# A two-layer hybrid block on one core: another order for the filters, twelve places for the second layer's expert weights, and branch products of split operands

## The reference

```python
def hyena_filter_spectrum(n, w1, b1, freq, w2, b2, w3):
    ...
    hh = jnp.sin(fr * (z @ w1.astype(f32) + b1.astype(f32)))
    hh = jnp.sin(fr * (hh @ w2.astype(f32) + b2.astype(f32)))
    hh = (hh @ w3.astype(f32)).reshape(n, HY_ORDER, 2, BRANCH_WIDTH)
    hh = hh * jnp.exp(-t * deltas)[:, None, None, :]
    fwd, bwd = hh[:, :, 0], hh[:, :, 1]
    buf = jnp.concatenate([fwd, jnp.zeros((1, HY_ORDER, BRANCH_WIDTH), f32), bwd[:0:-1]], axis=0)
    buf = buf / jnp.sum(jnp.abs(buf), axis=0, keepdims=True)
    return jnp.fft.rfft(buf, axis=0)

def merge_branches(p, y_attn, pool_w, pool_scale, hy_params, w_branch, w_out):
    ...
    gates = jax.nn.sigmoid(p[..., GATE_OFF:].astype(jnp.float32)).reshape(b, n, N_BRANCH, D_MODEL)
    ys = jnp.stack([y_attn.astype(p.dtype), y_pool, y_hy], axis=2)
    br = jnp.einsum('blnc,ncd->blnd', ys, w_branch, preferred_element_type=jnp.float32)
    merged = jnp.sum(gates * br, axis=2).astype(p.dtype)
    return merged @ w_out

def grouped_moe(h, w_router, router_bias, w_gate, w_up, w_down):
    ...
    for e in range(N_EXPERTS):
        hid = jax.nn.silu(h @ w_gate[e]) * (h @ w_up[e])
        out = out + gates[:, e:e + 1] * (hid @ w_down[e]).astype(jnp.float32)
```

## Time and profile before

| | |
|---|---|
| device time, three runs | 1842.62 median (1838.25 to 1848.77) |
| the profiled execution's own time | 1845.94 |
| its span | 1844.2 |
| mean granted clock of TensorE | 0.916 |
| TensorE busy | 1546.9 (84%) |
| VectorE, ScalarE, GpSimd busy | 819.1 (44%), 605.2 (33%), 357.9 (19%) |
| loaded and stored | 374.29 MB, mean 203 GB/s |

### The profile page before, as it was taken

One profiled execution on the slowest core, in us unless ns is written; L12 is line 12 of the kernel. 1 busy time (PEld: TensorE's weight loads), 2 busy tenths in 40 slices (PEclk: granted clock), 3 DMA queues, 4 the chain that ended last, 5 costly groups with the idle time before them and its releaser, 6 DMA issues. The chain is left out here.

```text
span 1844.2 us, 19309 instructions
## 1 busy us (share of the span) xinstructions
PE 1546.9 (84%) x7556; PEld 1071.5 (58%) x7556; DVE 819.1 (44%) x1204; ACT 605.2 (33%) x830; POOL 357.9 (19%) x206
## 2 busy tenths in 40 slices
PE   5898997789999977999999766789889987777872
PEld 1365676556666646788888334468678973222322
DVE  2621666751111245889899444144853433000102
ACT  2322222351111242787877124122242331000002
POOL 0132332112222301101010112335124540000000
PEclk8799999799999986999999787889899997999996
DMA  7456321102242305899999722753205446999992
GB/s 247 134 206 239 124 65 52 43 1 69 68 137 68 114 25 217 323 405 405 408 407 368 292 87 83 295 183 99 73 10 179 161 138 229 420 421 422 422 398 80
DMA packets 118416, 374.29 MB, mean 203 GB/s; under 512 B 8222, under 2 KB 70880, under 8 KB 87360
## 3 DMA queue, kind: packets, MB, share of 16 engines
q1 hardware_dynamic: 107584, 334.58, 48.1%
q0 software_dynamic: 10752, 38.61, 5.5%
HBM read 356.39 MB, written 16.78 MB: 202 GB/s over the span
## 5 line engine op out<-in xcount | busy, mean ns | idle before, releaser
L587 POOL TENSOR_TENSOR w_lo<-ring,w_hi 128x1024 fp32r<-128x1024 f32 x120 | 288.7, 2418 | 724.0 <-ACT w_hi L1328 724.0
L705 PE MATMUL bank<-h_hi,w_hi 128*128 128x512 f32 (+1 forms) x896 | 329.8, 368 | 35.3 <-DVE h_lo L1609 21.2
L706 PE MATMUL bank<-h_hi,w_lo 128*128 128x512 f32 (+1 forms) x896 | 311.6, 348 | 0.0
L707 PE MATMUL bank<-h_lo,w_hi 128*128 128x512 f32 (+1 forms) x896 | 311.5, 348 | 0.0
L705 PEld LDWEIGHTS bank<-h_hi,w_hi 128*128 128x128 f32 x896 | 176.3, 197 | 84.9 <-issue 44.6
L706 PEld LDWEIGHTS bank<-h_hi,w_lo 128*128 128x128 f32 x896 | 177.0, 198 | 23.2 <-issue 5.0
L707 PEld LDWEIGHTS bank<-h_lo,w_hi 128*128 128x128 f32 x896 | 176.2, 197 | 20.2
L1328 ACT ACTIVATE w_hi<-ring 128x1024 fp32r<-128x1024 f32 x120 | 125.2, 1052 | 107.9 <-DMA ring<-in_w_in 76.1
L705 PE MATMUL bank<-w_hi,h_hi 128*128 128x512 f32 (+1 forms) x384 | 142.1, 370 | 9.8 <-DVE w_lo L1880 5.1
L1857 DVE SCALAR_TENSOR_TENSOR mix<-mix,bank 128x512 f32<-128x512 f32 (+1 forms) x48 | 26.6, 554 | 262.3 <-PE bank L985 165.4
L706 PE MATMUL bank<-w_hi,h_lo 128*128 128x512 f32 (+1 forms) x384 | 138.8, 362 | 0.0
(11 more groups left out here) (260 smaller groups left out, 2326.9 us busy)
## 6 DMA issues: line engine op xcount, KB each, us to landing
ring<-in_w_up_e SPq DMA_DIRECT2D x54, 1024.0 KB, 8.2
ring<-in_w_in SPq DMA_DIRECT2D x52, 1024.0 KB, 7.0
mix<-in_w_gate_e SPq DMA_DIRECT2D x52, 1024.0 KB, 8.4
ring<-in_w_mod SPq DMA_DIRECT2D x48, 1024.0 KB, 7.2
mix<-in_w_down_e SPq DMA_DIRECT2D x34, 1024.0 KB, 8.9
ring<-in_w_down_e SPq DMA_DIRECT2D x30, 1024.0 KB, 7.8
ring<-in_w_branch SPq DMA_DIRECT2D x12, 1024.0 KB, 5.2
ring<-in_w_gate_e SPq DMA_DIRECT2D x12, 1024.0 KB, 8.6
```

What stands on the lines that cost most here:

```text
L587: pool.tensor_tensor(w_lo[:, slot], rview(raw, 8)[:, :, x * P:(x + 1) * P], w_hi[:, slot].bitcast(F32), ALU.subtract).then_inc(w_l, 1)
L705: first = mm(dst, stat[0], mov[0], start=start, stop=False)
L706: mm(dst, stat[1], mov[0], start=False, stop=False)
L707: return first, mm(dst, stat[0], mov[1], start=False, stop=stop)
```

## The change

**1. The order of the filters.** At the start SyncE loads the filter's inputs first (with semaphores of their own), and TensorE does both `filter_in` and order 0's product ahead of the norm's sums; the `mod` steps follow with `spectra_a(0, 0)` between the fourth and fifth, mod columns before `spectra_b`. Order 1's rest comes after the second and the third tile. Between the layers order 1 leaves the chain ahead of the transposes: its product now comes after them, `spectra_a` after the norm's sums, `spectra_b` after the second layer's first tile. It has areas of its own for this (`late_fpm`, `late_fraw`, `late_fhid`).

**2. Places.** `XS = [6, 12]`: the second layer's experts have twelve places. The six new ones lie in the split operands' memory (`h_hi`, `h_lo`, `w_hi`, `w_lo`), which is unused in these experts; pieces 3 to 9 wait for the last residual of the output projection, 10 and 11 for the router's products.

**3. The merge.** A branch product is three one-pass products of split operands. ScalarE copies the mixer's output of a branch (`ys_hi`, 128x2048, or 128x1024 in the second layer) and, for each half, the piece of branch weights (`wb_hi`, 128x2048); VectorE subtracts both, the weights in place in the ring. TensorE waits for these subtractions (`g_yl`, `g_wl`) and no longer for the load. The memset goes, branch 0 writes `merged` directly, and ScalarE's and VectorE's loops are written out.

```diff
-XS = 6
+XS = [6, 12]
...
+        ys_hi = mix_r[:, 10240:16384].rearrange("p (n c t) -> p n c t", n=3, c=BK)
+        ys_lo = mix_r[:, 0:6144].rearrange("p (n c t) -> p n c t", n=3, c=BK)
+        wb_hi = mix_r[:, 20480:22528]
...
+        idle = [plain[:, i * 2048:(i + 1) * 2048] for i in (4, 5, 6, 7, 0, 2)]
+        xraw = [[ring[:, i] for i in range(RS)] + (idle if l else []) +
+                [area(o, 2048) for o in ((17408, 19456, 0), (2048, 17408, 19456))[l]] for l in range(DEPTH)]
...
+                elif l and c < XS[l] - 2:
+
+                    sp.wait_ge(o_d[l], 16 * l + 8 * streams(l))
+                elif c < XS[l] - 1 or l:
...
                             for k in range(BK):
-                                last = mm(bank[2 + m % 2][:, 0:T], rview(bslot, 4)[:, k, r * P:(r + 1) * P],
-                                          ys[:, bass.ds(n, 1), k, 0:T], start=k == 0, stop=k == BK - 1)
+                                w = [v.rearrange("p (k n) -> p k n", k=BK)[:, k, r * P:(r + 1) * P]
+                                     for v in (wb_hi, ring_r[:, bslot])]
+                                y = [v[:, bass.ds(n, 1), k, 0:T] for v in (ys_hi, ys_lo)]
+                                first, last = mm3(bank[2 + m % 2][:, 0:T], w, y, k == 0, k == BK - 1)
...
                             gate(w_u if m == 4 else None)
+                            if m == 0:
+                                pe.wait_ge(g_yl, n + (3 * l + 1))
                             if r == 0:
-                                pe.wait_ge(ring_full[bslot], n * (16 * 6 // RS) + full_at(b_at))
+                                pe.wait_ge(g_wl, n * 2 + (6 * l + h + 1))
...
+                        if m % 4 == 0:
+                            at = at_of[("merge", l, 6 * n + 3 * (m // 4) + 1)]
+                            act.wait_ge(ring_full[at % RS], full_at(at))
+                            if n + m:
+
+                                act.wait_ge(g_pe[l], 2 * DK * n + 2 * m - 1)
+                            A(wb_hi, ring[:, at % RS], ACT.Copy).then_inc(g_wh, 1)
...
-                V.memset(merged, 0.0).then_inc(g_d[l], 2)
-                dve.wait_ge(g_d[l], 2)
-                with dve.Fori(0, 3) as n:
+                dve.nop().then_inc(g_d[l], 2)
...
+                        if m % 4 == 0:
+                            slot = at_of[("merge", l, 6 * n + 3 * (m // 4) + 1)] % RS
+                            dve.wait_ge(g_wh, 6 * l + 2 * n + m // 4 + 1)
+                            V.tensor_tensor(ring_r[:, slot], ring[:, slot], wb_hi.bitcast(F32), ALU.subtract
+                                            ).then_inc(g_wl, 1)
```

More of the change, by code:

```diff
@@ L257, in build @@
         s_ldl = sems("layer_params_loaded")
-        s_ldf = sems("filter_tables_loaded")
+        s_ldf = both("filter_tables_loaded")
+        s_lds = sem("filter_transforms_loaded")
         ring_full = [sem(f"ring_full{i}") for i in range(RS)]
@@ L333, in build @@
         x_hh = sem("expert_in_leading")
-        x_full = [sem(f"expert_weights_loaded{i}") for i in range(XS)]
+        x_full = [sem(f"expert_weights_loaded{i}") for i in range(XS[0])]
         x_wh = sem("expert_weights_leading")
@@ L467, in _ @@
         def _(sp):
-            for dst, name in ((cc[:, 0, :], "c_cols"), (square[:], "square"), (par[0][:], "par0"),
-                              (xT[:], "x_cols")):
-                sp.dma_start(dst, a[name]).then_inc(s_ld, 16)
             def slot_free(at):
@@ L805, in _ @@
                 if l:
+                    filters(l, 1)
                     norm_pe(2 * l, NT)
+                    spectra_a(l, 1)
                 def proj_tile(g):
@@ L1211, in _ @@
                     pe.wait_ge(x_yd[l], 16 * l + NS)
-                    filters_and_mod(l + 1)
-                    spectra_a(l + 1, 1)
-                    spectra_b(l + 1, 1)
-                    pe.wait_ge(f_a[l + 1], 6 * l + 12)
-                    pe.wait_ge(f_d[l + 1], 10 * l + 20)
+                    filter_in(l + 1, 0)
+                    mods_and_filters(l + 1, range(DK))
+                    pe.wait_ge(f_a[l + 1], 6 * l + 10)
                     pe.wait_ge(m_tk[l + 1], 3 * l + 4)
@@ L1222, in _ @@
                 for k in range(DK):
+                    if k == DK - 1 and l + 1 < DEPTH:
+                        pe.wait_ge(f_d[l + 1], 10 * l + 16)
                     for j in range(nt):
@@ L1700, in _ @@
                 if l:
+                    taps(l, 1)
                     norm_dve_root(2 * l, NT)
@@ L1862, in _, with parts_in @@
-                chain[0] += 3 * DK
+                dve.nop().then_inc(g_d[l], 2)
+                def parts_in(n):
+                    dve.wait_ge(g_yh, 3 * l + n + 1)
+                    V.tensor_tensor(ys_lo[:, n, :, 0:T], ys[:, n, :, 0:T], ys_hi[:, n, :, 0:T].bitcast(F32), ALU.subtract
+                                    ).then_inc(g_yl, 1)
+                parts_in(0)
+                for n in range(3):
+                    for m in range(DK):
+                        if m % 4 == 0:
[3 more added lines that the diff above has]
+                                            ).then_inc(g_wl, 1)
+                        dve.wait_ge(g_t[l], 3 * DK * l + n * DK + m + 1)
+                        dve.wait_ge(g_pe[l], n * (2 * DK) + 2 * m + 2)
+                        gated = merged[:, m, 0:T] if n == 0 else mtmp[:, 0:T]
+                        last = V.scalar_tensor_tensor(gated, gate_t[:, m % 2, 0:T], 1.0, bank[2 + m % 2][:, 0:T],
+                                                      ALU.add, ALU.mult)
+                        if n:
+                            link(last)
+                            last = V.tensor_tensor(merged[:, m, 0:T], merged[:, m, 0:T], gated, ALU.add)
+                        last.then_inc(g_d[l], 1)
+                        dve.wait_ge(g_d[l], n * DK + m + 3)
+                        if m == 1 and n < 2:
+                            parts_in(n + 1)
```

226 lines of the change are left out of this document (126 added, 100 removed).

## The result

The changed kernel takes 1800.1 us (median of 6 runs, 1789.9 to 1803.9), the kernel before 1844.5 (6 runs, 1838.3 to 1848.8): 0.9749 of its time, 95% interval 0.9715 to 0.9783. The forecast was 1782, range 1760 to 1812: the direction and the range hold, the size does not; 44 us were won where 61 were forecast. The profiled execution of the changed kernel is its fastest run, 1789.9 (span 1787.8), so beside the 1845.9 of before it shows a gain of 56 and hides most of the miss.

A forecast was written before the change was run, and what follows sets the result against it. Bounds were taken as small-step waits at the start and between layers, full TensorE in the merges, and full DMA in the second layer's experts. Terms summed to −60.7 from 1845.9: 1785.2 profiled, 1782 as median, range 1760 to 1812.

The forecast's parts named there:

- Merge, first layer: First layer's merge: a branch falls from 3.47 to 2.73, 24 times, −17.8; first splits cost +1.1; memset priced separately, −3.5.
- The cover: First layer's merge: load, copy and subtraction for each later half, 10.3 us, fit under two gates, 10.9; costed at nothing.
- Merge, second layer: Second layer's merge: split chain of 9.7 against cover of 5.8, each half stalls 3.9; +2.9 with memset, clock another +5.
- Twelve places: Second layer's experts: six more weight pieces load while the DMA engines are idle in the routing, −14.9.
- Start: Start, up to the first product after the third projection tile: new filter order moves it from 111.66 to 96.1, −15.5.
- Between the layers: Between the layers: transposes 28.6 earlier; product step and taps cost 3.6, last spectra step 7; −18.
- signs of being wrong: Start's mark above 104, a split of 4 us or more in either merge, or last experts' idle gone at unchanged length.
- rival G: Merges: GpSimd holds up VectorE's subtractions, +12 in the second layer and +9 in the first, 1803; chance 0.12.
- C: Start and between the layers: landing of weights sets the pace, new filter order gives nothing, +33.5, 1815; chance 0.11.
- B: Second layer's merge: split chain mostly covered, merge no longer than now, −7.5 and no clock loss, 1770; chance 0.10.
- D: Second layer's experts: twelve places give nothing, as TensorE or expert inputs become the bound, +14.9, 1797; chance 0.08.
- E: Second layer's merge: TensorE stays at 1.2 GHz, clock below about 0.63, up to +104, decides from +60; chance 0.03.

The follow-up runs named there:

- the FP32 experiment: Changed kernel with FP32 branch products and no splits in both layers: ratio 0.975; merge and output of the first layer take 283.0 us.
- the repeat: The changed kernel measured again without any edit: median 1799.9 us, ratio 0.978 to the kernel before.
- the experiment: Under twelve places: the changed kernel with six places in both layers, 1815.0 us against 1799.9 for the changed kernel beside it.
- the old-order kernel: Changed kernel with the filter order of before, at the start and between the layers; twelve places and split merge stay: 1814.0 us, ratio 0.982.

## Why the forecast was right, and where it missed

In range, 18 us too low. Step by step, with gains as the table's traces show them:

- **Merge, first layer**: forecast −17.8 + 1.1, measured −18.5 (284.2 to 265.7), and 17.3 by the stretch in the FP32 experiment. The cover held, by 10.3 against 10.9 as worked out. The memset is 4.2, forecast 3.5: from attention's last product to the first gate 6.24 became 2.07. What the trace priced was right: 24 times the measured 0.74 gives this result, and 24 times the 0.87 named beside it would be 3 more.
- **Merge, second layer**: forecast stalls of 3.9; measured 3.90, 3.04, 3.96, 3.16, 3.96. The cause is shown: shorten the chain alone and 23 us go. A half of 21.2 was forecast, 22.4 measured, since the clock's part is inside. Merge, memset and clock together were to cost +2.9 + 5 = +7.9; in the two traces they cost 11.8 − 4.2 = +7.6, and in the repeat 10.9. That the number fits is partly luck. The forecast has the split cost 11.4 (7.9 and the memset's 3.5); against FP32 products in the same kernel it costs 18.7 by the medians, and 15 to 21 by the traces. The first half, where a gain was forecast, stalled 1.98. What hides the difference is a gain of 3.5 to 6.5 that the forecast did not have: by so much FP32 products in the changed kernel beat the kernel before in this merge.
- **Twelve places**: forecast −14.9 (6 times 2.5 is 15.0), measured −16.4 between the traces and −15.1 by the experiment.
- **Start**: forecast −15.5 at the mark, measured −5.4 between the two traces. Seven traces of the new order have the mark at 100.7 to 107.0 (mean 105.2), the two of the old order at 111.7 and 113.3. At the end of attention 1 the two of the old order stand at 394.4 and 399.5, the seven of the new between 386.6 and 394.2 (mean 390.9): −6. The step that failed is "the eight mod steps with spectra_a, paced by three ring places refilled every 5.2 us, to 52.5; mod columns 1.3, the spectra_b step 5.5". The mod steps began 8.6 later than before (34.06 against 25.49) behind the filter and the norm's sums, so two refills were waited for in the open (3.31 and 3.32), and spectra_b took 9.5 at the lower clock. The sum also drops the second filter's product step: it was ahead of the first tile (64.31, 6.55 long), the forecast takes it away there and adds it nowhere. It is still ahead of the first tile, and 75.86 − 71.39, that is 4.5 of it, lies behind the readiness of `h_lo` (70.70 + 0.69). And its own terms give 97.0 for the mark (111.66 less 8.9, 3.2 and 2.5), not 96.1. The experiment that pulls three mod steps forward brings 10 of the missing us back by its ratio, 4 to 5 of them seen by the end of attention.
- **Between the layers**: forecast −18. Between the two traces it came: 201.6 from `filter_in` to the pooling products became 182.0, −19.6. But the trace of before is the longer of the two with the old order and that of the changed kernel the shortest of ten. Against the old-order kernel, term by term: the transposes are 25.5 earlier (28.6 forecast), the product step and taps cost 7.2 (3.6 forecast), and the last spectra step 9 (7). Net −9 with that shortest trace, −5 with the mean of ten. So two things failed. The base was one trace, with a clock of 0.78 in this stretch, taken as if every run had it; how often the kernel before has it is not shown, and its profiled run as a whole (1845.9) is an ordinary one beside its median of 1844.5. And the product step, the taps and the last spectra step were priced too low, the last one because it stood in front of no wait and ran at the lower clock; the experiment that moves it wins 9.

With +2.2 from the mark to the end of attention 1 and −2.1 in attention 2, the terms of the two traces add up to the 56 that they show. From 56 down to the 44 of the medians are 10.2 by which the profiled run of the changed kernel lies below its median, and 1.4 by which that of the kernel before lies above its own. Where those 12 sit by stretch one trace can't tell, but the experiments say which part is short: of the 33.5 forecast for the filter order 8 to 14 came.

Two of the forecast's own signs of being wrong came true and are to be counted against it. The mark at the start stands above 104 (106.30, and in six of the seven traces), which was the sign for the start's term. And a split took 4 or more in a merge (VectorE's 4.35 at 411.81): the collision of rival G is there, but in the first layer, where nobody waited for it.

Of the rivals, C was partly right: most of the filter order's gain did not come, and waits on mod weights were part of why. B, D and E fell, and G fell by its price. E had its mechanism, the clock behind a stall, though it cost single stretches and never the merge: 0.96 and 0.94 there, not 0.63.

## What to carry to other kernels

Count a reordering by the waits that it fills. A step moved into a wait for weights won 9 us here, about its own length at the lower clock. A step moved out of a wait was paid in full, 3.7 of the 6 us that were lost. When operands are split on the way to TensorE, the chain of load, copy and subtraction must be shorter than the cover. Splitting it in the order of use took the wait from 3.9 to 1, and no cost of it shows in the first layer, where it was not needed (266.2 to 267.7 against 265.7 to 267.4). And what a stretch takes at a low clock differs from trace to trace of the same code, so take its length from several traces before costing against it: a forecast and its check by one trace each can both be flattered.

## What the runs showed of the hardware that I had not expected

Idle times of 3 to 4 us cost more than themselves: waits of 16.7 in sum taken away made the merge 21.4 shorter (23.1 by the medians). Behind 3.90 of waiting the next products of 256 columns were 0.21 apart instead of 0.12, and the clock from 1338 to 1342 was 0.50; with waits of 1 the merge's clock was 1.00 instead of 0.96. The runs of this kernel, 1790 to 1807, order themselves mostly by their mean clock (0.927 to 0.915). Inside a run the clock of a stretch is not fixed by the code. The same eight records of the first filter's product between the layers, in the same kernel, took 3.70 in one trace (at 1009.54, three mod steps ahead of the norm's sums) and 7.19 in its repeat (at 1012.71). The stretch from `filter_in` to the first tile there took 68.3 to 73.1 in eleven traces of the same code, at clocks of 0.86 to 0.76. A VectorE subtraction of 128x2048 beside a GpSimd one took 4.35, alone 2.29.
